# A hybrid mixer on one core: the state-space scan between the two halves of a convolution, and its output rows first

## What is computed

```python
proj = u @ w_in
conv_in, z, xbc, dt_raw = jnp.split(proj, [s0, s1, s2], axis=-1)
ya = conformer_conv(conv_in, conv_dw_w, conv_dw_b, conv_ln_g, conv_ln_b)
yb = mamba2_ssd(z, xbc, dt_raw, ssm_conv_w, ssm_conv_b, ssm_dt_bias, ssm_a_log, ssm_d, ssm_norm_g)
return jnp.concatenate([ya.astype(u.dtype), yb.astype(u.dtype)], axis=-1) @ w_out
```

## Time and profile before

| | |
|---|---|
| time, median of 3 runs | 3427.25 us (3426.72 to 3432.38) |
| the profiled execution, its own time | 3426.4 us |
| its span | 3424.5 us |
| busy: PE, PEld, DVE, ACT | 3207.8, 2687.2, 2267.4, 1869.3 us |
| mean granted TensorE clock | 0.966 of full speed |
| the mixer in the trace | about 223 to 490 us of the span |

### The profile page before, as it was taken

How to read it: one execution, slowest core, us unless ns; L and a number is a source line. 1 busy time by engine, 2 the same in 40 slices (tenths; PEclk the granted TensorE clock), 3 DMA queues, 4 the chain that set the end, 5 groups by cost and what they waited for, 6 DMA issues and landing times.

```text
span 3424.5 us, 42058 instructions
## 1 busy us (share of the span) xinstructions
PE 3207.8 (94%) x15980; PEld 2687.2 (78%) x15980; DVE 2267.4 (66%) x2672; ACT 1869.3 (55%) x2447; POOL 14.4 (0%) x26
## 2 busy tenths in 40 slices
PE   6999689999999979999899899996999999999997
PEld 5887478878887867888688788885888788788885
DVE  4549755555455555666554647655898898898897
ACT  4441344454455434655444446463777677677774
POOL 0000000000000000000000000000000000000000
PEclk9999789999999989999899999997999999999999
DMA  8543145554534444444455344333999899899993
GB/s 272 165 149 141 49 154 184 196 178 159 154 124 167 159 148 160 173 147 148 151 191 183 129 159 159 137 128 142 344 363 350 325 362 357 323 360 360 345 360 143
DMA packets 381146, 719.06 MB, mean 210 GB/s; under 512 B 14009, under 2 KB 153727, under 8 KB 380831
## 3 DMA queue, kind: packets, MB, share of 16 engines
q1 hardware_dynamic: 376368, 707.71, 58.1%
q0 software_dynamic: 2368, 8.52, 0.8%
q10 hardware_dynamic: 2223, 0.31, 0.1%
HBM read 715.44 MB, written 1.05 MB: 209 GB/s over the span
## 4 chain that ended last, share of the span: by engine, by line
PE 85%; DVE 8%; ACT 4%; issue 2%; DVEq 1%; DMA 0%; ACTq 0%; POOL 0%; SPq 0%
PE duo L981 13%; PE duo L983 13%; PE duo L982 13%; PE acc L981 8%; PE acc L983 8%; PE acc L982 8%; PE aux L981 2%; PE aux L983 2%; PE aux L982 2%; DVE arena L1736 2%; PE duo L542 1%; PE duo L543 1%; PE duo L544 1%; PE aux L542 1%; PE aux L544 1%
## 5 line engine op out<-in xcount | busy, mean ns | idle before, releaser
L1540 DVE TENSOR_TENSOR weights_split<-w,weights_split 128x1024 fp32r<-128x1024 f32 x672 | 792.1, 1221 | 122.3 <-ACT weights_split L1519 116.1
L1519 ACT ACTIVATE weights_split<-w 128x1024 fp32r<-128x1024 f32 x672 | 677.4, 1057 | 255.9 <-PE duo L983 180.3
L981 PE MATMUL duo<-weights_split,u_high 128*128 128x512 f32 x1776 | 705.4, 397 | 11.3 <-DVE weights_split L1540 8.1
L983 PE MATMUL duo<-weights_split,u_low 128*128 128x512 f32 x1776 | 695.1, 391 | 0.0
L982 PE MATMUL duo<-weights_split,u_high 128*128 128x512 f32 x1776 | 694.7, 391 | 0.0
L416 DVE TENSOR_TENSOR w_low<-w,w_high 128x1024 fp32r<-128x1024 f32 x312 | 378.1, 1223 | 355.2 <-ACT w_high L407 354.5
L1098 DVE TENSOR_TENSOR weights_split<-w,weights_split 128x1024 fp32r<-128x1024 f32 x320 | 377.7, 1222 | 283.0 <-ACT weights_split L1086 282.8
L407 ACT ACTIVATE w_high<-w 128x1024 fp32r<-128x1024 f32 x312 | 326.3, 1056 | 386.9 <-PE acc L983 122.8
L1086 ACT ACTIVATE weights_split<-w 128x1024 fp32r<-128x1024 f32 x320 | 322.3, 1058 | 255.9 <-PE duo L983 154.9
L981 PEld LDWEIGHTS duo<-weights_split,u_high 128*128 128x128 f32 x1776 | 336.0, 189 | 85.1 <-DVE weights_split L1540 8.9
L982 PEld LDWEIGHTS duo<-weights_split,u_high 128*128 128x128 f32 x1776 | 335.8, 189 | 70.8 <-issue 2.9
(11 more groups left out here) (394 smaller groups left out, 4978.2 us busy)
## 6 DMA issues: line engine op xcount, KB each, us to landing
w<-in_ffn_w_dram SPq DMA_DIRECT2D x132, 1024.0 KB, 7.6
w<-in_moe_w_gate_dram SPq DMA_DIRECT2D x112, 1024.0 KB, 7.0
w<-in_moe_w_up_dram SPq DMA_DIRECT2D x112, 1024.0 KB, 6.8
w<-in_moe_w_down_dram SPq DMA_DIRECT2D x112, 1024.0 KB, 7.9
w<-in_w_in_dram SPq DMA_DIRECT2D x92, 1024.0 KB, 7.1
w<-in_hyb_w_in_dram SPq DMA_DIRECT2D x18, 1024.0 KB, 7.3
w<-in_ffn_w_gate_dram SPq DMA_DIRECT2D x11, 1024.0 KB, 7.5
w<-in_ffn_w_up_dram SPq DMA_DIRECT2D x11, 1024.0 KB, 10.0
```

Of the source, the lines that this page charges most:

```text
L981: pe.matmul(bank_out, x_hi, w_hi, start=first, stop=False, skip_group_check=True)
L983: return pe.matmul(bank_out, x_lo, w_hi, start=False, stop=last, skip_group_check=True)
L1519: act.activation(units[:, place, 0, cut], src[:, cut], ACT.Copy).then_inc(sem("moe_high"), 1)
L1540: m = dve.tensor_tensor(units[:, place, 1, cut], src[:, cut], units[:, place, 0, cut], ALU.subtract)
```

## The change

The work of the stage is reordered, on all four engines:

- SyncE and TensorE: dt and xbc are multiplied right after g0 and v0, then g1 and v1. z comes last, in quarters of four matmuls (`z_quarters`), placed between the steps of the scan.
- VectorE: after the first half's taps come the 4 taps of xbc, dt and adt, and only then `gate_in(1)`. The 31 taps of the second half are cut into nine groups (`taps`), written out as single instructions instead of a loop (`dve_conv_taps`), and stand between the scan's steps; the last ten taps stand after y's normalization.
- The column sums and the products of B and C for both chunks are made at once, in banks 5 and 4. The copy of B transposed moves from ScalarE to VectorE.
- y's output rows come first and are plain: ScalarE copies the transposed y into `u`, 32 matmuls of 512 columns take the weights from the slots. Eight pieces on ScalarE and VectorE go away, as does y's split.
- The sum over the convolution's channels stands after the fifth of eight chunks of y's rows, the sum of squares after the last; the normalization of the convolution, its silu (now two chunks at a time, each split and handed over by itself) and its rows, split as before, end the stage.

```diff
+        def dve_conv_taps(key, since, upto, part):
+
+            w0 = stack_at("conv_dw_w")
+            for k in range(since, upto):
+                for c in part:
+                    if k == 0:
+                        m = dve.tensor_scalar(hc[:, c, :], cin[:, c, 0:T], pcol("conv_dw_w", c),
+                                              pcol("conv_dw_b", c), ALU.mult, ALU.add)
+                    else:
+                        dve.wait_ge(sem("conv_tap"), at("conv_tap", (key, k - 1, c)))
+                        m = dve.scalar_tensor_tensor(out=hc[:, c, :], in0=cin[:, c, k:k + T],
+                                                     scalar=par[:, w0 + 8 * k + c:w0 + 8 * k + c + 1],
+                                                     in1=hc[:, c, :], op0=ALU.mult, op1=ALU.add)
+                    m.then_inc(sem("conv_tap"), mark("conv_tap", (key, k, c)))
...
+            for name, i, _ in KEYS_A[2:]:
+                pe_cols_fm(u, ("A", name, i))
...
+            def z_quarters(i, *quarters):
+
+                key = ("A", "z", i)
+                for p in quarters:
+                    if p == 0:
+                        place[0] = arrived().rearrange("p (t n) -> p t n", n=COLS)
+                        pair_at[key] = 1
+                    b, t = pair_banks(key)[p // 2], p // 2
+                    if p % 2 == 0:
+                        claim(b)
+                    for k in range(4 * (p % 2), 4 * (p % 2) + 4):
+                        m = pe.matmul(bank(b), u[:, k, t * P:(t + 1) * P], place[0][:, k, :], start=(k == 0),
+                                      stop=(k == KC - 1), skip_group_check=True)
+                    if p % 2:
+                        m.then_inc(bank_full(b), fill(b, key))
+                if quarters[-1] == 3:
+                    released_last(f"bank_full{b}")
...
+            z_quarters(0, 0)
+            rows(0)
+            z_quarters(0, 1)
+            pe.wait_ge(sem("xds"), at("xds", "A"))
+            pe.wait_ge(sem("BT"), at("BT", "A"))
+            for g in range(2):
+                claim(2 + g)
+                m = pe.matmul(bank(2 + g), BT[:, g * P:(g + 1) * P], xds[:, g * 512:(g + 1) * 512],
+                              start=True, stop=True)
+                m.then_inc(bank_full(2 + g), fill(2 + g, ("A", "state")))
+            z_quarters(0, 2, 3)
+            diagonal(0)
+            rows(1)
+            z_quarters(1, 0, 1)
+            pe.wait_ge(sem("state"), at("state", 1))
+            for g in range(2):
+                claim(2 + g)
+                m = pe.matmul(bank(2 + g), xc[:, 10 + g, P:T], state[:, g * 512:(g + 1) * 512],
+                              start=True, stop=True)
+                m.then_inc(bank_full(2 + g), fill(2 + g, ("A", "yoff")))
+            z_quarters(1, 2, 3)
+            diagonal(1)
             pe.wait_ge(sem("normed"), at("normed", ("A", "y", 1)))
             pe_to_fm(y, KC, ("A", "y"))
-            pe_block_rows(ybh, ybl, KC, "mixA", ("A", "y"), start=False)
+            claim(0, 1, 2, 3)
+            for k in range(KC):
+                if k % 4 == 0:
+                    slot = arrived().rearrange("p (t n) -> p t n", n=D)
+                if k % 2 == 0:
+                    pe.wait_ge(sem("fm_ready"), at("fm_ready", (("A", "y"), k // 2)))
+                for t in range(NT):
+                    for half in range(2):
+                        m = pe.matmul(acc[:, 2 * t + half, :], u[:, k, t * P:(t + 1) * P],
+                                      slot[:, k % 4, half * 512:(half + 1) * 512], start=(k == 0), stop=False,
+                                      skip_group_check=True)
+                if k % 4 == 3:
+                    m.then_inc(bank_full(3), mark("bank_full3", ("A", "rows", k)))
+                    released_last("bank_full3")
+                if k == 4:
+                    pe.wait_ge(sem("conv_tap"), at("conv_tap", ("A half 1", TAPS - 1, 7)))
+                    claim(4)
+                    for c in range(8):
+                        m = pe.matmul(bank(4)[:, 0:T], cst("ones"), hc[:, c, :], start=(c == 0), stop=(c == 7),
+                                      skip_group_check=True)
+                    m.then_inc(bank_full(4), fill(4, ("A", "sum")))
+            pe.wait_ge(sem("squared"), at("squared", "A"))
+            claim(5)
+            for c in range(8):
+                m = pe.matmul(bank(5)[:, 0:T], cst("ones"), sq_c[:, c, :], start=(c == 0), stop=(c == 7),
+                              skip_group_check=True)
+            m.then_inc(bank_full(5), fill(5, ("A", "sumsq")))
+            pe_block_rows(yah, yal, KC, "mixA", ("A", "ya"), start=False)
...
         def dve_mixer_a():
...
-            gate_in(1)
...
-            dve_conv("conv_tap", "A", hc, cin, 8, TAPS, "conv_dw_w", "conv_dw_b", range(4, 8))
...
+            gate_in(1)
...
+            taps(0, 5)
...
+            differences(0)
+            taps(5, 7)
+            weighted(0)
+            for t in range(NT):
                 V(dve.tensor_tensor(split(y[:, t, :], 16), split(xs[:, t, :], 16), bc(dskip, 2, h64), ALU.mult))
-                for b in range(2):
-                    dve.wait_ge(bank_full(4 + b), filled_at(4 + b, ("A", "ydiag", t)))
...
+            taps(7, 11)
+            diagonal(0)
+            taps(11, 13)
+            differences(1)
+            taps(13, 15)
+            weighted(1)
...
+            taps(15, 19)
+            gated(0)
+            diagonal(1)
+            gated(1)
+            taps(19, 21)
...
-            dve_feed(6)
-            dve_to_fm_split(("A", "y"), gain=lambda c: pcol("ssm_norm_g", c), high=ybh, low=ybl)
+            taps(21, TAPS)
+            dve_feed(2)
...
+            for x in range(2):
+                part = slice(4 * x, 4 * x + 4)
+                dve.tensor_tensor(hc[:, part, :], hc[:, part, :], bc(var_c, 1, [P, 4, T]), ALU.mult)\
+                   .then_inc(sem("scaled_c"), mark("scaled_c", ("A", x)))
+            for c in range(0, KC, 2):
+                dve.wait_ge(sem("fm_high"), at("fm_high", (("A", "ya"), c // 2)))
+                dve.tensor_tensor(yal[:, c:c + 2, :], ya[:, c:c + 2, :], yah[:, c:c + 2, :], ALU.subtract)\
+                   .then_inc(sem("fm_split"), mark("fm_split", (("A", "ya"), c // 2)))
...
-                    load(*[col_block(w, c) for _, _, c in KEYS_A])
+                    load(*[col_block(w, c) for _, _, c in KEYS_A[0:2]])
                     sp.wait_ge(sem("h_ready"), at("h_ready", ("mixA", "pre")))
                     sp.dma_start(wdt[:, :, :], w[:, 4608:4624].rearrange("(t p) n -> p t n", p=P))\
                       .then_inc(sem("wdt_landed"), 16)
                     load(*[col_block(w, 3072 + 512 * i) for i in range(3)])
+                    load(*[col_block(w, c) for _, _, c in KEYS_A[2:]])
                     load(*[col_block(w, 2048 + 512 * i) for i in range(2)])
-                    load(*[row_block(a["hyb_w_out"][0], 512 * i) for i in range(4)])
+                    load(*[row_block(a["hyb_w_out"][0], 512 * i) for i in (2, 3, 0, 1)])
                 elif key == "mixB":
```

More of the change, by code:

```diff
@@ L1760, in build @@
         xs = view(18708, NT, 1024)
-        cbm = view(20756, 2, P)
         BT = view(21012, 256)
@@ L1822, in pe_mixer_a, with rows @@
+            def rows(t):
                 for b in range(4):
@@ new lines, in pe_mixer_a @@
+            pe.wait_ge(sem("xbc_ready"), at("xbc_ready", 11))
+            pe.wait_ge(sem("adt"), at("adt", "A"))
+            claim(5)
+            for t in range(NT):
+                for i, name in enumerate(("upper", "ones")):
+                    pe.matmul(bank(5)[:, 256 + 32 * i + 16 * t:256 + 32 * i + 16 * t + 16], cst(name),
+                              adt[:, 16 * t:16 * t + 16], start=True, stop=True)
+            for g in range(2):
+                m = pe.transpose(bank(5)[:, g * P:(g + 1) * P], xc[:, 8 + g, 0:P], cst("ident"))
@@ new lines, in dve_mixer_a @@
+            for t in range(NT):
+                dve.wait_ge(sem("xs"), at("xs", ("read", 2 * t + 1, ("A", "xs", t))))
+                V(dve.tensor_tensor(split(xdt[:, t, :], 16), split(xs[:, t, :], 16), bc(dt[:, 16 * t:16 * t + 16], 2, h64),
+                                    ALU.mult))
+            dve.wait_ge(sem("dse"), at("dse", "A"))
+            dve.tensor_tensor(split(xds, 16), split(xdt[:, 0, :], 16), bc(dse, 2, h64), ALU.mult)\
+               .then_inc(sem("xds"), mark("xds", "A"))
```

291 lines of the change are left out of this document (125 added, 166 removed).

## The result

| | before | after |
|---|---|---|
| median of 3 runs | 3427.25 us | 3394.38 us (3391.61 to 3397.42) |
| profiled execution, its span | 3426.4, 3424.5 us | 3397.42, 3395.6 us |
| mean granted clock | 0.966 | 0.970 |
| ScalarE's next step (line 667) starts at | 490.3 us | 458.45 us |

The change is faster: the ratio is 0.990, 95% interval 0.9877 to 0.9922, that is 27 to 42 us of 3427, the medians 32.9 apart. Two executions of the later sets, one of the kernel before (5440 us) and one of a variant (6254 us), fell into a slow state and are left out of every median and ratio. The forecast was 3402, a gain of 24.8; in the profile the stage ends 31.9 us sooner.

The account below looks back on a forecast made before the run. TensorE bounds the kernel, but the mixer loses time to VectorE's taps, then handovers. Projections, VectorE's chain, rows, clock and tail end the stage at 465.5 against 490.3: gain 24.8 us, 3402 predicted, range 3394 to 3418.

Parts of the forecast that it names:

- the clock: Half clock after TensorE's pauses: 3.5 us in y's rows and 4.0 in ya's, 7.5 in all.
- rival 2: Clock returns soon, taps lose nothing: clock terms shrink from 7.5 to 1.8, handovers' 1.5 go; 3395 us; chance 0.14.
- v1: TensorE's projections end with v1 at 326.5; VectorE waits 4.9 us for it and goes on at 327.3.
- VectorE's chain: VectorE's instructions from 327.3 to normalized y: 61.3 us plus 1.5 for handovers, ending at 390.1.
- TensorE's stations: TensorE's scan products come before VectorE asks: row sums 338 for 340.4, diagonals 354 for 358 and 377.5 for 382.
- Rival 1: Handovers stay: a late z quarter or silu delays VectorE at six stations, some 2 us each; +12, 3414; chance 0.21.
- rival 3: First tap group covers nothing: stations slip 3 to 4 us each or taps run at 0.48; 3421, no change; chance 0.06.
- rival 4: TensorE at half clock through y's plain rows and both sums: 31.5 us more, 3434, slower; chance 0.04.
- rival 5: A weight block comes late for v1 or y's rows; no chance of its own, left in rival 3's.
- Transposes: Four rounds of y's transposes and ScalarE copies ahead of y's rows: 4.0 us, ending at 394.1.
- sums and last chunks: Within y's rows: sum over channels 3.6 us, last three chunks 10.4, sum of squares 3.6.
- tail: Exposed normalization of the convolution between the sum of squares and ya's rows: 6.5 us, ending at 439.1.

Follow-up runs that it names:

- the run without pauses: The changed kernel plus unread matmuls in TensorE's two pauses, 23 ahead of y's transposes and 13 ahead of ya's rows: 3393.2 us, ratio 0.9897 to before.
- the repeated run: The changed kernel run once more, unaltered: 3395.6 us, ratio 0.9908 to the kernel before.
- z ahead: Against the changed kernel, both blocks of z stand whole between v1 and the scan's transposes: 3418.3 us, ratio 0.997 to before.
- the taps ahead: Against the changed kernel, all 31 taps of the second half stand in one piece ahead of the scan: 3437.5 us, ratio 1.0029 to before.

## Why the prediction was wrong, step by step

The direction and the mechanism held: the experiments put the gain in VectorE's idle time, under z's cover, with the plain rows as a condition (10 us without them). The time was 8 us too high, and the step that failed is **the clock**: "I take 3.5 for the pause before y's rows", and 4.0 for ya's. Measured against the run without pauses, they are 0.2 and 1.6 (0.5 and 1.7 in the repeated run). I took half of a stretch of 16 us at half clock as the upper end and a value between the bounds. But in that stretch TensorE ran two state products and then the scan's small ones; behind the pauses of the change stand transposes and matmuls of 512 columns, and there the clock was full again after 3.1 us of work (ya's rows with z ahead) to 6.3 (y's transposes with the taps ahead), the extremes of these runs where the work went on without a gap. For ya's rows I had read 1.9 off the trace, which was near; the 3 to 3.5 "ahead of them" were diagonal products (430.68 to 437.5) that no longer stand there. That the kind of work makes the difference is my reading; the runs show the cases, not the cause. Two more rows fit it: with z ahead, diagonal products and row sums ran from 373.0 and the clock was half until 385.2; before the change it was half through the diagonal products from 430.68 and full 3.9 us into ya's rows.

The nearer row was the window of y's rows, 0.96, which I had as the lower bound of 0.9. That is rival 2, whose 3395 was the result; its mechanism (clock soon back, no handovers) is what the traces show, while that its number came so close owes something to chance, since v1 (+1.3), the sum of VectorE's instructions (-0.8) and the later stages (+2.9) were in it no better than in mine.

Three slips of the text change nothing in the sum: 303.5, 17.4 and 0.4 make 321.3 and not 321.6; a list of 50 us from 326.5 ends at 376.5 and not 377.5; and in the stretch of the earlier trace rows TensorE was busy from 404.84 and not only from 409 (its timeline before the change):

```profile
404.84 3.78 PE L1835 MATMUL aux<-arena 128*128 128x512 f32 x4 [6.14 <-DVE arena L2004]
```

The other terms, forecast to measured:

- **v1**: the gating's end forecast at 327.3, measured 328.6, although the start lay 0.3 us earlier. "Five blocks x 13.8" overlooked a clock cost in the other direction: behind dt's matmuls of 16 columns the first block of xbc took 15.5 us, with the clock at 0.69, 0.50 and 0.96 in the windows from 256 to 262. The trace of before had it, hidden beside VectorE's taps, in TensorE's timeline right behind the row of dt:

```profile
285.07 15.42 PE L387 MATMUL duo<-u,w 128*128 128x256 f32 x64
```

- **VectorE's chain**: 62.8 with handovers, 60.5 measured. The taps ran at 0.40 us, as in the loop, and the 1.5 us for handovers were not there: no idle row stands between 327.9 and 389. The other 0.8 is spread over all kinds, by the starts of the rows: 33.0 for the taps (33.2 forecast), 9.0 for 2048 columns (9.2), 2.3 for the minima (2.5), 2.8 for the small ones (3.0).
- **TensorE's stations**: as forecast. Second diagonal done at 378.4 (377.5), each 3.7 us (3.5), and it held 1.4 us of wait for VectorE. Rival 1 did not come about, nor rival 3, whose slips of 3 to 4 us a station would stand in the same rows; rival 4's half clock lasted about 4 us, and no block of weights landed late (rival 5).
- **Transposes** 3.8 (4.0), **sums and last chunks** 17.3 (17.6), **tail** 6.6 (6.5): held. ya's rows 24.3 (26.4), the clock again.

In sum: v1 +1.3, chain -2.3, y's first rows -3.6, ya's -2.1, the rest -0.4: some 7 us less, from the forecast end of 465.5 to the measured 458.45. The execution gained 29.0 rather than 31.9 us, so 2.9 were lost again in later stages.

The Trainium skill ("TensorE: Matmul & The Clock Gate", Part 1) says: "For modeling, the ramp penalty is <1% of a typical kernel span; don't fit to a specific cold count." That it can be left out was my reading of this. Left out, it gave a gain of 32, and 32.9 was measured. The run with filled pauses shows why that was close: 2.7 us of clock stand on the path, 1.0 of them already in the transposes' 4.0. I had written that the rows speak against the page; they did not: 2.7 us is 0.08% of the span, and my own 7.5 us (0.2%) would have been within its 1% too.

## What to carry to other kernels

When independent work fills one engine's waits, write down both engines' lists by stations: VectorE's 61 us against TensorE's 50 told that the gain would hold, and also where it would end: with 5 us taken off VectorE's chain it waited for TensorE at the second diagonal (0.18 us). Price a clock ramp by the row whose work *after* the pause is like yours, and look for rows in covered stretches (15.4 us behind dt) before using the clean ones. And compare an edit by its own stage as well as by the whole time, since a kernel's other stages can move by more than the edit, and compare times with the kernel before in the same set of runs (its medians lay between 3423.5 and 3427.6).

## What was unexpected

- The experts' stage, untouched by every edit, took 1048 to 1065 us. It repeated for the three kernels that were profiled twice (1053.6 and 1053.9; 1053.9 and 1053.6; 1064.9 and 1065.2); the 1048 of two kernels were seen once each. One matmul more or less in the mixer, 2000 us earlier, took out or put in two waits of TensorE of over 7 us.
- Behind 32 matmul records of 16 columns the granted clock fell to 0.50 for 3.4 us though TensorE had not paused: some 1.6 us in the next block, before and after the change.
- The pause's length did not set how soon the clock was back: behind 10.8 us it took 4.1 us of work (4.8 in the repeated run), behind 7.3 us 6.0 and 6.1 in two kernels, behind 5.8 us 3.9 in one kernel and 6.3 in another.
